# Down projection ended bank by bank, and attention operands split straight from PSUM, in a two-block transformer kernel

## What is computed

```
h = rms_norm(x) * (1 + scale) + shift                # first block
q, k, v, glu_a, glu_b, gates = split(h @ w_in + b_in)    # q, k, v: 8 heads of 64
scores = q k^T * 64**-0.5 + bias ...                 # first attention, with a 31-tap convolution beside it
...
y = (gelu(gate) * val) @ w_down                      # w_down: 2816 x 1024
x = x + gt_f * rms_norm(y, g_post_ffn)               # the residual behind the down projection
u = rms_norm(x, norm_g)                              # second block, first layer
q, k, v, z = split(u @ a_w_in)                       # 1024, 256, 256, 1024 columns
```

## Time and profile before

| | |
|---|---|
| median of 3 runs | 1576.48 us (1576.16 to 1577.61) |
| profiled execution | 1576.45 us |
| its span, first to last instruction | 1574.7 us |
| TensorE busy | 1457.8 us, 93% |
| VectorE busy | 968.1 us, 61% |
| ScalarE busy | 727.4 us, 46% |
| GpSimd busy | 227.2 us, 14% |
| mean granted TensorE clock | 0.968 of full |

### The profile page before, as it was taken

One profiled execution on the slowest core, in us unless ns is written; L12 is line 12 of the kernel. 1 busy time (PEld: TensorE's weight loads), 2 busy tenths in 40 slices (PEclk: granted clock), 3 DMA queues, 4 the chain that ended last, 5 costly groups with the idle time before them and its releaser, 6 DMA issues. The chain is left out here.

```text
span 1574.7 us, 19710 instructions
## 1 busy us (share of the span) xinstructions
PE 1457.8 (93%) x6850; PEld 1149.3 (73%) x6850; DVE 968.1 (61%) x1513; ACT 727.4 (46%) x1249; POOL 227.2 (14%) x218
## 2 busy tenths in 40 slices
PE   5899899979978999999998999998999979999996
PEld 3687677768746888887885687776777758888775
DVE  5669777467665565554223637986463467888554
ACT  4424554553334454544113426775442446666442
POOL 3104633231110000000000000111110011232111
PEclk9999899989998999999999999999999999999998
DMA  9532233225511323222221322112222120000321
GB/s 387 208 106 81 77 123 129 98 107 201 199 42 56 104 85 101 89 98 94 95 94 65 101 81 74 50 59 94 81 84 90 54 80 28 28 28 25 111 93 53
DMA packets 39881, 151.65 MB, mean 96 GB/s; under 512 B 4784, under 2 KB 4928, under 8 KB 39040
## 3 DMA queue, kind: packets, MB, share of 16 engines
q1 hardware_dynamic: 29664, 105.92, 19.6%
q0 software_dynamic: 10144, 44.76, 7.7%
HBM read 144.37 MB, written 6.29 MB: 96 GB/s over the span
## 5 line engine op out<-in xcount | busy, mean ns | idle before, releaser
L629 PE MATMUL ps<-a_hi,w_hi 128*128 128x512 f32 x880 | 361.2, 410 | 19.9 <-ACTq L1346 11.8
L631 PE MATMUL ps<-a_hi,w_lo 128*128 128x512 f32 x880 | 349.8, 398 | 0.0
L630 PE MATMUL ps<-a_lo,w_hi 128*128 128x512 f32 x880 | 349.8, 398 | 0.0
L1522 DVE TENSOR_TENSOR w_lo<-w_raw,w_hi 128x1024 fp32r<-128x1024 f32 x130 | 169.2, 1304 | 159.0 <-ACT w_hi L1065 158.4
L629 PEld LDWEIGHTS ps<-a_hi,w_hi 128*128 128x128 f32 x880 | 166.9, 190 | 64.1 <-ACTq L1346 12.7
L631 PEld LDWEIGHTS ps<-a_hi,w_lo 128*128 128x128 f32 x880 | 166.6, 189 | 40.7
L630 PEld LDWEIGHTS ps<-a_lo,w_hi 128*128 128x128 f32 x880 | 167.0, 190 | 35.5 <-issue 0.5
L1065 ACT ACTIVATE w_hi<-w_raw 128x1024 fp32r<-128x1024 f32 x138 | 144.5, 1048 | 76.2 <-PE ps L631 57.4
L629 PE MATMUL ps<-b_hi,w_hi 128*128 128x512 f32 x240 | 97.1, 404 | 7.4 <-DVE b_lo L1935 5.5
L631 PE MATMUL ps<-b_hi,w_lo 128*128 128x512 f32 x240 | 95.1, 396 | 0.0
L630 PE MATMUL ps<-b_lo,w_hi 128*128 128x512 f32 x240 | 95.0, 396 | 0.0
(11 more groups left out here) (314 smaller groups left out, 3018.3 us busy)
## 6 DMA issues: line engine op xcount, KB each, us to landing
w_raw<-in_w SPq DMA_DIRECT2D x198, 512.0 KB, 3.5
ada_a<-in_ada POOLq DMA_DIRECT2D x16, 512.0 KB, 7.8
ada_g<-in_ada POOLq DMA_DIRECT2D x16, 512.0 KB, 3.8
ada_b<-in_ada POOLq DMA_DIRECT2D x16, 512.0 KB, 4.1
x_resid<-in_x POOLq DMA_DIRECT2D x2, 2048.0 KB, 11.9
pl_store<-pl_out POOLq DMA_DIRECT2D x2, 2048.0 KB, 9.0
pl<-pl_store POOLq DMA_DIRECT2D x2, 2048.0 KB, 9.4
alibi<-in_alibi POOLq DMA_DIRECT2D x16, 192.0 KB, 2.7
```

The lines of the kernel that those rows point to most:

```text
L629: pe.matmul(o, w[0], r[0], start=start, stop=False, skip_group_check=skip)
L630: pe.matmul(o, w[0], r[1], start=False, stop=False, skip_group_check=skip)
L631: return pe.matmul(o, w[1], r[0], start=False, stop=stop, skip_group_check=skip)
L1522: dve.tensor_tensor(w_lo[:, n % SLOTS, :], w_raw[:, n % RAW, :], w_hi[:, n % SLOTS, :].bitcast(F32), ALU.subtract).then_inc(w_lo_done, 1)
```

## The change

Four edits. (1) First attention: queries and keys are split straight from the bank. ScalarE writes `qk_hi` from PSUM with the bias, VectorE `qk_lo` from PSUM after the three taps; `tmp` is not used. The factor 1/8 of the queries moves into their four weight chunks (`chunk_scale`) and into a scaled copy of the bias (one new small instruction). (2) `token_tiles` waits for each bank just ahead of its first matmul. (3) The last three chunks of the down projection are held, and used for one output bank after the other, 7 down to 0 (`down_out`); copies, squares and GpSimd's additions follow bank by bank; two sums of squares remain. (4) Behind it VectorE writes `a_lo` tile by tile within the residual and also adds the squares (`summed_square`); the first four query tiles advance together, feature tile by feature tile (`first_queries`), with the two sums of `norm_a` after the second. The splits of the `a_q` chunks move: one before the copies, one behind them, two into the residual; from there on the splits are four chunks ahead. The banks of the query tiles count as free with the write of `tmp`.

```diff
-        LT["a_q"] = plan(KT, R["q_a"])
+        tmps_a = tmps_ahead + H1 // 2 + 2 * KT + FT
+        LT["a_q"] = plan(KT, tmp_w, tmps_a)
...
-            used_at[CH["down"] + j] = (down_step, j + 1)
+            used_at[CH["down"] + j] = (down_step, j + 1) if j < FT - 1 else (down_out, KT)
...
+        def chunk_scale(n):
+            return HD ** -0.5 if CH["qk"] <= n < CH["qk"] + CT else 1.0
...
+            for k in range(KT):
+                add_square("down", k)
...
             def token_tiles(tile, chunk, n_chunks, src, width, kt):
-                banks = [free_bank(tile + t) for t in range(NT)]
+                banks = [ps[:, (tile + t) % LIN, :] for t in range(NT)]
...
                         for t in range(NT):
+                            if k == 0:
+                                free_bank(tile + t)
...
-            for k in range(FT - 4, FT):
-                down(k, CH["down"] + k + 1, (CH["down"] + k) % SLOTS, False, k == FT - 1, k + 1)
-            for k in range(KT):
-                if k == 0:
-                    pe.wait_ge(R["y_d"], 1)
-                square_sum(k, KT)
-            pe.wait_ge(R["y_d"], KT)
-            for k in range(KT):
-                square_sum(k, KT)
-            tiles("a_q", KT, A, R["in_a"])
+            down(FT - 4, CH["down"] + FT - 3, (CH["down"] + FT - 4) % SLOTS, False, False, FT - 3)
+            for f in reversed(range(KT)):
+                for k in range(FT - 3, FT):
+                    if f == KT - 1:
+                        pe.wait_ge(w_lo_done, CH["down"] + k + 1)
+                        pe.wait_ge(R["g"], k + 1)
+                    slot = (CH["down"] + k) % SLOTS
+                    m = mm3(ps[:, f, :], cols((w_hi[:, slot, :], w_lo[:, slot, :]), P * f), (g_hi[:, k, :], g_lo[:, k, :]),
+                            False, k == FT - 1)
+                    if k == FT - 1:
+                        m.then_inc(down_out, 1)
+                    elif f == 0:
+                        m.then_inc(down_step, 1)
+            pe.wait_ge(R["y_d"], 1)
+            added_squares("down")
+            def first_queries(j, k):
+                pe.wait_ge(R["in_a"], k + 1)
+                w = weights(CH["a_q"] + j)
+                return mm3(ps[:, (LT["a_q"] + j) % LIN, :], cols(w, P * k), (a_hi[:, k, :], a_lo[:, k, :]), k == 0, k == KT - 1, skip=True)
+            for j in range(LIN):
+                free_bank(LT["a_q"] + j)
+            for k in range(KT - 2):
+                for j in range(LIN):
+                    first_queries(j, k)
+            for j in range(LIN):
+                first_queries(j, KT - 2)
+                first_queries(j, KT - 1).then_inc(lin_done, 1)
+                if j == 1:
+                    added_squares("norm_a")
+            tiles("a_q", KT - LIN, A, first=LIN)
...
-                hi_of_tmp(qk_hi[:, f, :])
+                act.wait_ge(lin_done, LT["qk"] + f + 1)
+                act.activation(qk_hi[:, f, :], ps[:, (LT["qk"] + f) % LIN, :], ACT.Identity, bias=qk_bias(f)).then_inc(hi_done, 1)
...
-            for k in range(3 + (FT - 6) // 4 * 4, FT):
-                split(CH["down"] + k + WEIGHT_LEAD)
+            split(CH["a_q"])
             ln_exp_set()
             for k in range(KT):
-                square(y_d[:, KT - 1 - k, :], R["y_d"], k + 1)
+                square(y_d[:, KT - 1 - k, :], R["y_d"], k + 1, k)
+                if k == KT - 2:
+                    split(CH["a_q"] + 1)
+            split(CH["a_q"] + 2)
             rsqrt(D)
...
             for k in range(KT):
-                scaled_input(a_hi, "norm_a", k, R["x_ffn"], k + 1)
+                act.wait_ge(R["x_ffn"], k + 1)
+                act.activation(a_hi[:, k, :], x[:, k, :], ACT.Identity, scale=v("norm_a", k)).then_inc(hi_done, 1)
+                square(x[:, k, :], R["x_ffn"], k + 1, k)
+                if k == 0:
+                    split(CH["a_q"] + 3)
+            split(CH["a_q"] + LIN)
             rsqrt(D)
...
-                slot = tmp_slot()
-                scale = HD ** -0.5 if f < 4 else 1.0
-                dve.tensor_scalar(slot, src, v("b_in", f), scale, ALU.add, ALU.mult).then_inc(tmp_w, 1)
-                conv_taps(QK_TAPS)
-                lo_of_tmp(qk_lo[:, f, :], qk_hi[:, f, :], R["qk"])
+                dve.wait_ge(hi_done, his[0])
+                dve.scalar_tensor_tensor(qk_lo[:, f, :], src, qk_bias(f), qk_hi[:, f, :].bitcast(F32), ALU.add, ALU.subtract
+                                         ).then_inc(R["qk"], 1)
...
-            dve.wait_ge(down_step, FT)
+            split(CH["a_q"])
             for k in range(KT):
+                dve.wait_ge(down_out, k + 1)
+                if k == 0:
+                    dve.wait_ge(down_step, FT - 3)
                 dve.tensor_copy(y_d[:, KT - 1 - k, :], ps[:, KT - 1 - k, :]).then_inc(R["y_d"], 1)
+            split(CH["a_q"] + 1)
             dve.wait_ge(R["y_d"], KT)
...
-            residual(y_d, range(KT), 3, R["x_ffn"])
+            r = wait_rs()
+            dve.wait_ge(gains, 4)
...
+            scaled_y(0)
             for k in range(KT):
+                dve.wait_ge(dve_step, steps[0])
+                dve.tensor_tensor(x[:, k, :], x[:, k, :], y_d[:, k, :], ALU.add).then_inc(R["x_ffn"], 1)
+                if k + 1 < KT:
+                    scaled_y(k + 1)
+                if k in (1, 2):
+                    split(CH["a_q"] + k + 1)
+                summed_square(k - 1)
                 scaled_lo(a_lo, a_hi, "norm_a", k, R["x_ffn"], k + 1, R["in_a"])
-            r = wait_rs()
             for f in range(KT):
-                split(CH["a_q"] + f + WEIGHT_LEAD)
+                split(CH["a_q"] + f + LIN)
```

More of the change, by code:

```diff
@@ L357, in build @@
         LT["v"] = plan(NT, R["v"])
-        tmps_ahead = KT + 8
+        tmps_ahead = KT
         tile1 = {}
@@ L1064, in split @@
                     act.wait_ge(*used_at[n - SLOTS])
-                act.activation(w_hi[:, n % SLOTS, :], w_raw[:, n % RAW, :], ACT.Copy).then_inc(w_hi_done, 1)
+                act.activation(w_hi[:, n % SLOTS, :], w_raw[:, n % RAW, :], ACT.Copy, scale=chunk_scale(n)).then_inc(w_hi_done, 1)
             def hi_of_tmp(dst, n=None):
@@ L1936, in scaled_lo, with scaled_y, summed_square @@
                                          ALU.subtract).then_inc(ready, 1)
-            residual(y_d, range(KT), 3, R["x_ffn"])
-            for k in range(KT):
+            r = wait_rs()
+            dve.wait_ge(gains, 4)
+            def scaled_y(k):
+                dve.scalar_tensor_tensor(y_d[:, k, :], y_d[:, k, :], gvec[:, KT * 3 + k:KT * 3 + k + 1], r, ALU.mult, ALU.mult
+                                         ).then_inc(dve_step, 1)
+                steps[0] += 1
+            def summed_square(k):
+                if 1 <= k <= KT - 2:
+                    dve.wait_ge(sq_ready, SQ["norm_a"] + k + 1)
+                    dve.wait_ge(sq_used, SQ["norm_a"] + k - 1)
+                    dve.tensor_tensor(sq[:, 0, :], sq[:, 0, :], sq[:, 1, :], ALU.add).then_inc(sq_used, 1)
+            scaled_y(0)
+            for k in range(KT):
+                dve.wait_ge(dve_step, steps[0])
[5 more added lines that the diff above has]
+                summed_square(k - 1)
                 scaled_lo(a_lo, a_hi, "norm_a", k, R["x_ffn"], k + 1, R["in_a"])
-            r = wait_rs()
             for f in range(KT):
-                split(CH["a_q"] + f + WEIGHT_LEAD)
+                split(CH["a_q"] + f + LIN)
+                if f == 0:
+                    r = wait_rs()
                 src = bank(LT["a_q"] + f)
@@ L1949, in _ @@
             for f in range(2):
-                split(CH["a_k"] + f + WEIGHT_LEAD)
+                if f:
+                    split(CH["a_k"] + f + WEIGHT_LEAD)
                 src = bank(LT["a_k"] + f)
```

26 lines of the change are left out of this document (20 added, 6 removed).

## The result

The changed kernel took 1556.59 us (median of 4 runs, 1556.21 to 1559.29), the kernel before 1577.05 in the same comparison (4 runs, 1576.16 to 1578.35): a ratio of 0.9873 with a 95% interval of 0.9856 to 0.989. The forecast was 1556.3, in a range of 1551.5 to 1563.

What follows compares the result with a forecast made beforehand. TensorE, busy 93% of the span, was taken as the bound. Gains of 7.9 (first attention), 11.2 (behind the down projection) and 1.0 (token_tiles again) sum to 20.1: 1576.4 - 20.1 gives 1556.3 us, range 1551.5 to 1563.

Steps and rivals of the forecast that it cites:

- (a): First attention, queries and keys from the bank: qk_lo falls from 1.23 to 0.69 us, a VectorE turn to 4.9.
- (b): token_tiles bank by bank, first attention: TensorE waits 0.4 us, attention starts 8.3 us earlier; 7.9 us gained with (a).
- R1: First attention: VectorE stays the limit, qk_lo and one tap stretched 0.55 us each; gain 4 us, time 1560; chance 0.12.
- Part one is passed on whole: The 7.9 us gained at the first attention reaches the end, since the attention behind it keeps TensorE full.
- (c): End of down projection: seven of eight copies beside matmuls; VectorE goes on 3.95 us behind the last matmul, 10.6 before.
- (d): Residual and first four query tiles: tiles end 35.6 us behind the last down matmul; 11.2 us gained with (c).
- (e): token_tiles again, wait of 1.94 us for the second key tile: three groups come first, 1.0 us gained, bounds 0 and 2.5.
- R2: First query tiles: a late load of the fourth query chunk passes on some 5 us; time 1561; chance 0.10.
- R5: Both places: no effect, because the waits only change places; time 1576; chance 0.02.
- R3: Larger gain: clock never falls in (d), v stage not stretched, 1.5 us more in (e); time 1552; chance 0.08.
- R4: Behind the down projection: TensorE's clock stays low after the sparse time; time 1583; chance 0.02.

Runs made afterwards that it cites:

- experiment 9: Changed kernel plus 20 unread matmuls in TensorE's wait behind the down projection; 1559.2 us, ratio 0.9896.
- Experiment 10: Changed kernel, but TensorE begins the up projection with the first input, not behind the eighth; 1553.09 us, ratio 0.9851.
- Experiment 6: Changed kernel, but the last three down chunks go chunk by chunk again, copies still bank by bank; 1566.56 us, ratio 0.9937.
- Experiment 7: Changed kernel, but only two down chunks held and the two query splits moved out of the residual; 1563.43 us, ratio 0.9918.
- p2: Kernel before with only the held down chunks and the residual with four query tiles together; 1563.14 us against 1576.99, ratio 0.9892.
- p4: Kernel before with only the bank-by-bank waits in token_tiles; 1576.13 us (10 runs), ratio 0.998.
- Experiment 5: Changed kernel, but the first four query tiles are made one after another; 1570.23 us, ratio 0.995.
- experiment 11: Changed kernel with the early up projection start, first tile held for five inputs, 38 unread matmuls meanwhile; 1557.1 us, ratio 0.9877.
- experiment 12: Changed kernel with the early up projection start and unread matmuls (20, 4 and 9) behind the down projection; 1552.04 us, ratio 0.9838.
- experiment 3: Kernel before with only the queries and keys split straight from the bank; 1575.04 us (10 runs), ratio 0.9978.

## Why the prediction was right

The total was right (1556.3 for 1556.59), and so was the order of its parts. But two of the terms were off, in opposite directions.

- **(a), (b):** right (the upper bound adds up to 181.7, not 181.9, which changes nothing). `qk_lo` fell to 0.74, TensorE waits 0.24 for the predicted 0.4, `v` ends at 177.74 for 177.4, the stop is 3.9 for 3.6, and the attention starts at 181.60 for 181.0, of which 0.6 is the later start of the stage. That VectorE's turn sets it was seen as well: turns of 5.1 us, between the 4.45 and the 5.55 of the two bounds. R1 fell: VectorE has those 6.7 us free.
- **"Part one is passed on whole":** not so in this profile. 7.7 us became 7.1 by the last `a_hi` (the forecast had priced 0.4 for the clock) and 5.7 at E. The step was an argument about which engine is full; it did not look at the stage where TensorE starts from an 11.8 us wait and where the number of matmuls at the low clock depends on the moment. In experiment 9, the same code up to there, all of 9.2 us reached E. Experiment 10 shows that more is to be had at this stage.
- **(c), (d):** right to half a us: 11.7 for 11.2. The scale came at E + 4.15 (3.95), the first `a_lo` ended at E + 7.2 (6.95), the last split at E + 12.7 (12.4). The sums cost some 1.7 instead of 1.9, and the low clock lay wholly in the time before the last split, so its 1.0 was not paid: the four tiles ended at E + 34.9 (35.6). What the prediction passed by is how near (c) is to its own edge: GpSimd's additions "every 2.1" were written down as hidden, and they are, but the chain of square and addition takes 2.07 of the 2.1. Experiments 6 and 7 show 9.0 and 6.9 us when it does not fit.
- **(e):** the mis-sized term, 3.1 for 1.0, outside its bounds of 0 to 2.5. Three groups moved in front of the wait as worked out (1.94 us of it became 0.68), and the rest, some 1.8, is the clock, which fell there before and no longer falls. Windows from the first `a_v` matmul to the second attention, before and then after:

```profile
933.60:952.90 19.30, 18.76 (x120) 17.33 (x120) 7.18 (x13) 3.67 (x7) 0.00 (x0) 0.91 0.18 60
```

```profile
916.00:932.50 16.50, 15.90 (x111) 14.37 (x111) 7.20 (x14) 3.88 (x7) 0.00 (x0) 1.00 0.23 73
```

I had put this case in as a bound, and taken the wait alone. That the clock's part may be luck as much as effect is seen in p2: without edit (2) it has the whole wait of 1.94 us, yet no low clock here (1.00 from 921.2 to 940.4), and gains 1.1 us. p4, with edit (2) alone, gains 3.1 like the change.
- **R2, R5:** no wait of ScalarE for the load of the fourth query chunk shows, and the waits did not only change places. **R3** is in part true: the clock's gain at (e) came, and the 1.0 of (d) too, though the clock did fall there; the `v` stage was stretched. **R4** did not happen in the change. Experiment 5, without the tiles side by side, has 23.9 us at the low clock, but most of them within the sparse time; in no profile did the clock stay low for more than some 4 us behind it.

So 7.9 + 11.2 + 1.0 was in truth 5.7 + 11.7 + 3.1 less 0.6 behind: two errors of about 2 us, both mostly of the clock, that cancelled. That the total came within 0.3 us is luck; that the two places give most of it, and which is the larger, is not.

Not tested apart are, within edit (4), the `a_lo` inside the residual, the additions of squares on VectorE, the earlier release of the banks and the lead of four chunks, and the new places of the splits.

## What to carry to other kernels

When outputs are finished bank by bank to hide what follows, hold as many chunks as make one bank's matmuls last as long as the slowest chain behind it; here three chunks (2.1 us) against a chain of square and addition (2.07); with two, and two splits moved, the kernel was 6.8 us slower. Where inputs trickle in after a serial stretch, let as many tiles advance together as there are banks: each input then feeds four groups of matmuls instead of one, and once all four weight chunks were split TensorE had no wait between them here. And a gain in front of a stage that starts from idle may or may not be passed on (5.7 of 7.7 us in one profile here, 9.2 of 9.2 in another of the same code): read the granted clock at the start of every such stage down the line, and begin the stage with its first input if nothing else forbids it.

## What the runs showed of the hardware

A TensorE that got one group of three matmuls every 2.5 us and waited 0.9 us of them stayed at the low clock, and got the full one back 3.2 us after the last of these waits, 23.9 us in all (experiment 5); one that got a group every 1.45 us had it back within 4 us (experiment 10). Matmuls whose output nobody reads ran at full clock and kept it up while they lasted (experiments 9, 11, 12), but in experiment 9 it fell 5.0 us after their end, in the second of two waits (0.8 and 2.1 us). The same code met its low stretches at different places from profile to profile, and so single edits of 2 us were hard to judge (experiments 3, 4, 11). VectorE's `qk_lo` (512 columns) took 0.74 us with one operand in PSUM, for 1.23 with both in SBUF, in the same stage beside GpSimd; the weight splits (1024 columns), both operands in SBUF, took 2.2 beside GpSimd and 1.22 without it.
